# The prompt's down product in seven block products instead of eight, with weight sums made by adding DMAs

## The reference, cut to what matters

```
h2 = rms_norm(x, lw['mlp_norm'])
x = x + jnp.square(jax.nn.relu(h2 @ lw['w_mlp_up'])) @ lw['w_mlp_down']
```

## Time and profile before

| | |
|---|---|
| median of 3 runs | 960.19 us (958.34 to 963.87) |
| profiled execution, its own time | 958.95 us |
| its span | 957.3 us |
| granted TensorE clock, mean | 0.995 |
| feed-forward part | about 563 us to the end |
| transfers | 118.34 MB, mean 124 GB/s |

### The profile page before, as it was taken

How to read it: one execution, slowest core, us unless ns; L and a number is a source line. 1 busy time by engine, 2 the same in 40 slices (tenths; PEclk the granted TensorE clock), 3 DMA queues, 4 the chain that set the end, 5 groups by cost and what they waited for, 6 DMA issues and landing times.

```text
span 957.3 us, 21321 instructions
## 1 busy us (share of the span) xinstructions
PE 922.2 (96%) x8818; PEld 782.3 (82%) x8818; DVE 555.7 (58%) x978; ACT 413.2 (43%) x701; POOL 30.9 (3%) x61
## 2 busy tenths in 40 slices
PE   5999999998999999899999999999999999999998
PEld 4999999988888577565656799878997899789976
DVE  6544576646757753855644844655853586358631
ACT  5335436312241666775445425522751275117610
POOL 0000001114300000000000000000000000000000
PEclk9999999999999999799999999999999999999999
DMA  8222213311202597358996322122222232213212
GB/s 263 67 66 69 66 66 104 105 53 50 81 5 71 176 324 260 131 195 284 358 390 222 110 89 89 45 88 84 93 89 89 69 108 88 88 56 121 88 45 99
DMA packets 63851, 118.34 MB, mean 124 GB/s; under 512 B 5182, under 2 KB 33438, under 8 KB 63754
## 3 DMA queue, kind: packets, MB, share of 16 engines
q1 hardware_dynamic: 60938, 111.68, 34.7%
q0 software_dynamic: 2816, 5.29, 1.6%
HBM read 110.41 MB, written 6.54 MB: 122 GB/s over the span
## 4 chain that ended last, share of the span: by engine, by line
PE 90%; DVE 6%; ACT 2%; DMA 1%; issue 1%; SPq 0%; DVEq 0%; ACTq 0%
PE PS L906 18%; PE PS L907 18%; PE PS L908 18%; PE PS L1067 7%; PE PS L1230 4%; PE PS L1557 3%; PE PS L1302 2%; PE PS L1252 2%; PE PS L934 2%; PE PS L1216 2%; PE PS L1338 1%; PE PS L1190 1%; PE PS L1207 1%; PE PS L1441 1%; PE PS L1444 1%
## 5 line engine op out<-in xcount | busy, mean ns | idle before, releaser
L906 PE MATMUL PS<-WH,U 128*128 128x512 f32 x256 | 101.3, 396 | 0.0
L907 PE MATMUL PS<-WL,U 128*128 128x512 f32 x256 | 99.8, 390 | 0.0
L908 PE MATMUL PS<-WH,U 128*128 128x512 f32 x256 | 99.6, 389 | 0.0
L906 PE MATMUL PS<-WR,HR 128*128 128x384 f32 (+1 forms) x192 | 66.5, 346 | 0.0
L1067 PE MATMUL PS<-AR 64*64 64x64 f32 x1912 | 61.7, 219 | 4.6 <-issue 2.3
L2663 DVE TENSOR_TENSOR VQ<-VQ,PS 128x512 f32<-128x512 f32 x40 | 27.4, 686 | 65.1 <-PE PS L908 65.0
L1067 PEld LDWEIGHTS PS<-AR 64*64 64x64 f32 x1912 | 58.5, 135 | 7.9 <-issue 5.2
L907 PE MATMUL PS<-WR,HR 128*128 128x384 f32 (+1 forms) x192 | 64.6, 336 | 0.0
L1901 ACT ACTIVATE WH<-Wraw 128x2048 fp32r<-128x2048 f32 x18 | 34.3, 1908 | 69.0 <-PE PS L908 68.9
L2680 DVE TENSOR_TENSOR WL<-Wraw,WH 128x2048 fp32r<-128x2048 f32 x18 | 41.3, 2293 | 36.7 <-ACT WH L1901 36.7
L1950 ACT ACTIVATE WH<-Wraw 128x1024 fp32r<-128x1024 f32 x24 | 25.4, 1059 | 83.7 <-PE PS L908 76.3
(11 more groups left out here) (399 smaller groups left out, 2143.6 us busy)
## 6 DMA issues: line engine op xcount, KB each, us to landing
AR<-in_cache_kv SPq DMA_DIRECT2D x120, 384.0 KB, 4.8
Wraw<-in_w_mlp_down SPq DMA_DIRECT2D x16, 1024.0 KB, 5.0
Wraw<-in_w_mlp_up SPq DMA_DIRECT2D x14, 1024.0 KB, 5.4
W<-in_w_in SPq DMA_DIRECT2D x6, 1536.0 KB, 6.6
QK<-in_cache_kv SPq DMA_DIRECT2D x8, 384.0 KB, 5.3
AR<-in_x_prompt SPq DMA_DIRECT2D x4, 512.0 KB, 5.4
Wraw<-in_w_out SPq DMA_DIRECT2D x2, 1024.0 KB, 6.9
VQ<-in_x_prompt SPq DMA_DIRECT2D x4, 512.0 KB, 5.9
```

Of the source, the lines that this page charges most:

```text
L906: mm(out, lH, rH, start=start, stop=False, skip_group_check=skip)
L907: mm(out, lH, rL, start=False, stop=False, skip_group_check=skip)
L908: return mm(out, lL, rH, start=False, stop=stop, skip_group_check=skip)
```

## The change

The prompt's down product of a round becomes one Strassen level: token halves a (256 rows), hidden halves jj (512), output halves n (512). Its seven pieces d multiply a form of the squared activations by a form of the weights. Four of the weight forms are sums of two to four blocks of `w_mlp_down`; they are made in device memory, in a tensor tau, by copying and by adding DMAs of 1 MB on POOL's queue, early in the program. The activation forms are summed by VectorE in place in the raw squares (`mix_sum`) and split (`mix_form_hi` on ScalarE, `mix_form_lo`). Weight forms are split in halves of 1024 columns (`half_hi`, `half_lo`). Piece products go to PSUM; VectorE takes pieces 0 and 5 into two tiles G (`take_common`) and adds the others to a quarter of x2. The samples' squares stand in `HL` with their high and low part side by side (128 columns) as the stationary operand, times the split weights, in pieces 0, 2, 3 and 4; VectorE adds both halves of the result (`take_samples`).

```diff
+            for r in range(2):
+                tau_copy(r, 1, down_block(r, 0, 0))
+                tau_copy(r, 3, down_block(r, 1, 1))
             for g in (2, 3):
                 pool.wait_ge(qk_normed, 5 * (g + 1))
...
+                if g == 2:
+                    for r in range(2, NR):
+                        tau_copy(r, 1, down_block(r, 0, 0))
+                        tau_copy(r, 3, down_block(r, 1, 1))
+                else:
+                    pool.wait_ge(tau_step, 16 * 2 * NR)
+                    for r in range(2):
+                        tau_add(r, 1, 0, 1)
+                        tau_add(r, 3, 0, 1)
...
+            for rows in (slice(32, 64), slice(64, 128)):
+                nc.gpsimd.memset(Call_rows[rows, :], 0.0).then_inc(rows_cleared, 1)
...
+            for r in range(2, NR):
+                tau_add(r, 1, 0, 1)
+                tau_add(r, 3, 0, 1)
+            pool.wait_ge(tau_step, 16 * 4 * NR)
+            for r in range(NR):
+                tau_copy(r, 2, tau_of(r, 1))
+            pool.wait_ge(tau_step, 16 * 5 * NR)
+            for r in range(NR):
+                tau_add(r, 2, 1, 1)
+            pool.wait_ge(tau_step, 16 * 6 * NR)
+            for r in range(NR):
+                tau_copy(r, 4, tau_of(r, 2))
+            pool.wait_ge(tau_step, 16 * 7 * NR)
+            for r in range(NR):
+                tau_add(r, 4, 1, 0)
             pool.wait_ge(rw_done, 1)
             pool.dma_start(o["wkv_prompt"], X4[:, 3648:3776]).then_inc(stored, 16)
```

SP issues 7 transfers of 1 MB for a down product instead of 4, and waits once for tau, ahead of the third feed-forward load:

```diff
             sp.wait_ge(o_ps, 10)
+            sp.wait_ge(tau_step, 16 * 8 * NR)
             for q in range(2, NM):
                 load_mlp(q)
```

TensorE's pieces (in `down`), with the waits between them:

```diff
+                def piece(d, banks, fresh, sample=None):
+                    pe.wait_ge(m_lo, 7 * r + d + 1)
...
+                    for h in range(2):
+                        pe.wait_ge(w_hi, split_at(r, d, h))
+                        pe.wait_ge(w_lo, split_at(r, d, h))
...
+                        for t in range(2):
+                            bank, c = banks + t, slice(t * 128, (t + 1) * 128)
+                            for k in range(2):
+                                last = mm3(...)
...
+                piece(0, X_BANK, True, sample=(0, 0))
...
+                piece(1, Q7_BANK, True)
+                pe.wait_ge(y_ready, 10 * r + 1)
+                piece(2, X_BANK, False, sample=(1, 0))
...
+                piece(3, Q5_BANK, True, sample=(0, 1))
+                pe.wait_ge(y_ready, 10 * r + 6)
+                piece(4, Q5_BANK, False, sample=(1, 1))
+                pe.wait_ge(y_ready, 10 * r + 4)
+                piece(5, X_BANK, True)
+                pe.wait_ge(y_ready, 10 * r + 3)
+                piece(6, Q7_BANK, False)
```

VectorE's order in a down stage (the start of `take_down`) and in the quads:

```diff
+            def take_down(r):
+                mix_form_lo(r, 2)
+                mix_sum(r, 2)
+                mix_sum(r, 3)
+                half_lo(r, 2, 0)
+                half_done(r, 0)
+                take_common(r, X_BANK, ADD if r else None)
+                half_lo(r, 2, 1)
+                take_samples(1, S_BANKS[0], SUB)
+                mix_form_lo(r, 3)
+                mix_sum(r, 4)
+                half_done(r, 1)
+                take_quarter(1, 1, Q7_BANK, SUB)
+                half_lo(r, 3, 0)
+                half_lo(r, 3, 1)
+                mix_form_lo(r, 4)
+                half_done(r, 2)
+                take_quarter(0, 0, X_BANK, ADD)
+                take_samples(0, S_BANKS[0], ADD)
+                half_lo(r, 4, 0)
+                half_lo(r, 4, 1)
+                mix_form_lo(r, 5)
+                half_done(r, 3)
+                take_quarter(1, 1, Q5_BANK, ADD)
...
+                    if j == 2:
+                        mix_sum(r, 1)
+                    if j == 3:
+                        mix_form_lo(r, 1)
                     partial_sums(i)
                     if j < 3:
                         for p in range(3):
                             form_lo(i + 1, p)
+                        if j == 2:
+                            mix_form_lo(r, 0)
```

More of the change, by code:

```diff
@@ L160, in build @@
         us = sb("us", [128, 36, NS])
-        U = sb("U", [128, 16, T], F32R)
+        with ExitStack() as early:
+            Uf = early.enter_context(nc.sbuf_tensor("Uf", [128, 16 * T], F32))
+        U = sb("U", [128, 16 * T], F32R)
         with ExitStack() as early:
@@ L771, in load_mlp @@
             def load_mlp(q):
[L772 to L780, removed]
+                if q >= 4:
+                    r, i = divmod(q - 2, 11)
+                    if r and i < 4:
+                        sp.wait_ge(s_lo, N_T + 4 * (4 * (r - 1) + i) + 3)
+                    else:
+                        done = split_at(r, i - 4, 1) if i >= 4 else i + 1
+                        sp.wait_ge(w_hi, done)
+                        sp.wait_ge(w_lo, done)
                 landed = in_up[q] if q < 2 else in_raw[q % 2]
@@ L847, in _ @@
         def _(pool):
+            ADD = ALU.add
             pool.wait_ge(shift_ev, 1)
@@ L1500, in quad @@
                 if j == 0:
[L1501 removed]
+                    pe.wait_ge(y_ready, 10 * (r - 1) + 9)
                 elif j == 1:
@@ new lines, in banks_of, with quarter, half_done, take_common @@
+            def banks_of(bank):
+                return PS[:, bank * 512:(bank + 2) * 512].rearrange("p (t c) -> p t c", t=2)
+            def quarter(a, n):
+                return x2[:, 2 * a:2 * a + 2, n * 512:(n + 1) * 512]
+            def half_done(r, d):
+                dve.wait_ge(dn_used, 14 * r + 2 * d + 2)
+            def take_common(r, bank, op):
+                for t in range(2):
+                    src = PS[:, (bank + t) * 512:(bank + t + 1) * 512]
+                    ins = copy(G[t], src) if op is None else tt(G[t], G[t], src, op)
+                ins.then_inc(y_ready, 1)
@@ L2860, in _, with add_common @@
                     form_lo(4 * r, 0)
+                half_done(r, 5)
+                take_common(r, X_BANK, SUB)
+                if r < NR - 1:
                     form_lo(4 * r, 1)
-                take_down(r, 1)
+                    half_done(r, 6)
+                    take_quarter(1, 0, Q7_BANK, ADD)
+            def add_common(a, n, op):
+                for t in range(2):
+                    x = x2[:, 2 * a + t, n * 512:(n + 1) * 512]
+                    ins = tt(x, x, G[t], op)
+                ins.then_inc(y_ready, 1)
@@ new lines, in _ @@
+            for n in range(8):
+                sample_low(n, n)
+                if n in (1, 3):
+                    split_lo(n // 2 + 2)
+                if n == 3:
+                    mix_sum(0, 1)
+                    mix_form_lo(0, 0)
+                if n == 4:
+                    mix_form_lo(0, 1)
+                if n in (5, 7):
+                    for h in range(2):
+                        half_lo(0, n // 2 - 2, h)
+                if n >= 4:
+                    turn_forms(n - 3)
@@ new lines, in _ @@
+            dve.wait_ge(y_ready, 10 * NR - 1)
+            add_common(0, 1, SUB)
+            add_common(1, 1, SUB)
+            add_common(1, 0, ADD)
+            dve.wait_ge(y_ready, 10 * NR + 2)
+            dve.wait_ge(dn_used, 14 * NR)
+            x = x2[:, 2, 0:512]
+            tt(x, x, PS[:, Q7_BANK * 512:(Q7_BANK + 1) * 512], ADD).then_inc(y_ready, 1)
+            dve.wait_ge(dn_used, 14 * NR + 1)
+            x = x2[:, 3, 0:512]
+            tt(x, x, PS[:, (Q7_BANK + 1) * 512:(Q7_BANK + 2) * 512], ADD).then_inc(y_ready, 1)
```

405 lines of the change are left out of this document (235 added, 170 removed).

## The result

Changed kernel: 970.27 us median of 4 runs (966.94 to 977.51); before, on the same chip: 959.79. Ratio 1.0131, 95% interval 1.0105 to 1.0157: slower, where 951 us was forecast. Measured once more beside other kernels it took 971.63, ratio 1.0153 (1.0080 to 1.0225). The profiled execution took 966.94 us with a span of 965.2; it is the fastest of the four.

The account below looks back on a forecast made before the run. TensorE, busy for 96% of the span, was taken as the bound. From the profiled execution, 958.95 - 26.1 + 17.4 - 0.6 = 949.7 us; the median of the runs is 1.2 higher: 951 us, range 938 to 978.

Parts of the forecast that it names:

- 24 matmuls a round fewer, samples cheaper, less the stalls and the end: Feed-forward part: TensorE saves 26.1 us (21.8 prompt, 4.3 samples), stalls return 17.4, the end saves 0.6.
- A round: Rounds 1 to 3: a share of the 26.1 us saved over four rounds, less stalls of 1.4 and 1.0 us.
- Piece 4 stops 1.4 us a round: Down product: piece 4 accumulates in piece 3's bank and waits until VectorE has taken it, 1.4 us per round.
- The fourth quad 1.0: Rounds 1 to 3: leftover form splits delay the Y sum that product 5 wants, 1.0 us per round.
- Piece 2 of round 0 5.6: Round 0's down product: piece 2 waits 5.6 us because VectorE's take into G stands behind the turned forms.
- The clock after it between 0 and 4, taken as 2: After round 0's stop before piece 2, a lower TensorE clock costs between 0 and 4 us, taken as 2.
- VectorE over 85% busy in down stages: Sign to look for in down products: VectorE has 39 of 45.4 us of work, so over 85% busy.
- What the DMAs add: Copies and adds on POOL's queue end near 375 us; 20 us of cover before VectorE's wait at 396.1, costed at nothing.
- a DMA share of 0.06 and 0.01 from 251 to 299: Profile rows before the change, cited against a late adding chain between 251 and 299 us.
- 5 taken, 5.8 named as the limit: Time of one 1 MB add on POOL's queue: 5 us assumed; at 5.8 us the cover before 396.1 us is used up.
- The sentence on the shared engines: Skill rule that POOL's and SP's transfers share 16 engines, so the cache pages are slowed as well; no size given.
- rival 1: Late adding chain makes VectorE wait at 396 us; each us of an add beyond 5.8 costs 24 us; chance 0.27.

Follow-up runs that it names:

- e1_no_tau: The changed kernel without its sixteen copies, sixteen adds and the waits for them, loading plain blocks instead of the sums: 948.17 us.
- e6_one_at_a_time: The changed kernel with each of the twenty transfers from 253 us on waiting until the one before has landed: 998.82 us.
- e10_paced_all: e9_paced with round 0's fourth turned form made after the down product's splits, and pieces 4 and 5 exchanged: 939.55 us.
- e3_early: The changed kernel with all 32 transfers moved ahead of the recurrent stage, first copies at 24 us: 963.80 us.
- e5_by_need: The changed kernel with some 215 to 561 us free of transfers, both sides filled, SP waiting for each sum only before its own load: 953.40 us.
- e9_paced: e5_by_need with the early twelve transfers put back where the change had them: 954.06 us.

## Why the prediction was wrong

Its feed-forward part stands step by step:
- *24 matmuls a round fewer, samples cheaper, less the stalls and the end*: -26.1 + 17.4 - 0.6 = -9.3 us; part 2 shrank by 8.6.
- *A round*: 4.1 us less forecast for rounds 1 to 3 (26.1 / 4 - 2.4); the first up loads of rounds 1, 2 and 3 were issued 96.55 us apart before, 92.57 and 92.75 after, 4.0 and 3.8 less.
- *Piece 4 stops 1.4 us a round*: 1.3. *The fourth quad 1.0*: 0.5 of wait, 0.7 in the length of the four quads. *Piece 2 of round 0 5.6*: 4.9. *The clock after it between 0 and 4, taken as 2*: TensorE's next matmuls start 0.43 us apart until 651.3 us, where a later pair is 0.23, that is 1.2 instead of 2.4 GHz for 5.7 us after the stop, 2.7 us.

```profile
647.44 0.63 PE L959 MATMUL PS<-WL,U 128*128 128x512 f32 x1
647.87 0.63 PE L960 MATMUL PS<-WH,VQL 128*128 128x512 f32 x1
...
652.00 0.39 PE L958 MATMUL PS<-WH,U 128*128 128x512 f32 x1
652.23 0.39 PE L959 MATMUL PS<-WL,U 128*128 128x512 f32 x1
```

- *VectorE over 85% busy in down stages*: 40.15 of 47.2 us in round 1's, from 728.2 to 775.4, 85%; forecast 39 of 45.4.

**The step that failed is "What the DMAs add", costed at nothing.** It asked who waits for the chain, and answered that rightly: the wkv stores, with cover to 396 us; they were issued at 341.5, q0 was busy with the last adds until about 380 (done near 375 forecast), and VectorE's list has no wait for them. It took for the traffic's price only what stands behind it in a queue. The rows it leaned on, a DMA share of 0.06 and 0.01 from 251 to 299, were read as room. But the same engines carry TensorE's instruction packets, one in 4 us, and the 2.3 us of issue waits that before shows there were not read as theirs. Measured: 9 to 17 us in the recurrent stage, up to 10 at the pages, 24 in all by the ratios. An add of 6.7 us (5 taken, 5.8 named as the limit) made the chain longer than assumed, but with adds turned into copies 18 of the 22 us (by the medians, against e1_no_tau) were still lost.

The sentence on the shared engines stood there ("by it the pages are slowed as well"), and no term was given to it: the pages' loads rose from 4.8 to 5.7 us to landing, and one wait of 6.6 us followed. The rival 1 (0.27 for the slower side) had the sign and the cause's name but another place; e6_one_at_a_time shows what its place would have looked like. Its time of 975 for an add of 6.8 us is near the result by chance only: at the 6.7 us measured its formula puts some 20 us at VectorE's wait, where there was none.

What stays open: why the recurrent stage loses 9 us in one execution and 17 in another with the same transfers beside it, whether other engines' instruction loads are delayed too, and why a packet comes late when the engines are busy for two thirds only. That the delayed packets are the cause was read from their times beside TensorE's gaps; no run moved the packets alone.

## What to carry to other kernels

Before sending bulk transfers through a stretch because its DMA share is low, look at how many instructions per microsecond the busiest engine issues there: at 28 small matmuls per us the sums cost 9 to 17 us for some 70 us of transfers; at 6.6 per us, from 155 to 203 us in e10_paced_all, nothing (the one stop of 2.4 us in e3_early is the exception seen). Look also for short issue waits that are already there. Place them by who would be late (first loads of a stage, small matmuls, page loads), and give each consumer its own wait; in e10_paced_all they were then free within the noise, while each of e5_by_need and e9_paced, placed a little otherwise, lost 4 to 6 us. When a profile and a forecast differ, cut both spans at one common event first; here that told at once that the rewritten part was right.

## What the runs showed of the hardware

- 1 MB from device memory to device memory: 3.7 us a copy, 6.7 an add in groups of four; beside the page loads 4.2 and some 10. The ratio of the first two is 1.8. The Trainium skill states 1.93, measured between a collective that copies and one that adds, for two source reads (Collectives: The Full Stack, section on the bandwidth ceiling); the trace is near it.
- Instructions come in 16 KB packets, some 253 of TensorE's to a packet, through the same engines. Beside the sums a packet came up to 8 us after the one before (279.0 to 287.0) instead of 4 to 5, and TensorE resumed some 2.5 us behind it. Limiting the bulk transfers to one outstanding (share 0.66 instead of 0.97) did not help.
- A stop of 4.9 us was followed by 5.7 us at 1.2 GHz; stops of 1.3 us, with full work around them, by none that shows in the spacing of the matmuls.
